# Expert layers of a diffusion trunk: row buffers handed over pair by pair from the one-hot columns, and the first eight key blocks' gates kept on the chip

## Chip, cores and metric

The kernel is one program on one core of a Trainium2 chip. The metric is the device time in microseconds (us) of one execution, as the median of several. The profile is of one execution of its own.

## What is computed

Two layers of a trunk over 640 tokens (128 context, 512 latent) of width 1024. Each layer has a mixer (not touched here) and then an expert layer with product keys:

```python
q = (xt @ w_q).reshape(n, 8, 2, 128)
s = einsum('thcd,hcnd->thcn', q, keys)            # 128 keys a side
sv, si = top_k(s, 16)                             # 16 best of each side
best, bi = top_k(sv[:, :, 0, :, None] + sv[:, :, 1, None, :], 16)   # 16 best pairs of each of 8 heads
eidx, gate = i1 * 128 + i2, softmax(best)         # 128 experts a token
act = gelu(einsum('td,ted->te', xi, u_tab[eidx])) * gate
out = einsum('te,ted->td', act, v_tab[eidx])
```

`u_tab` and `v_tab` have 16,384 rows of 1024 floats each.

## The kernel before

The five token tiles of 128 are treated in two ways. The first 320 tokens (`DENSE`) are **dense**: all 128 blocks of 128 experts pass through the chip. For each block `c`, TensorE makes the dot products (`chunk_dots`, L608), ScalarE the gelu (`gelu`, L451), VectorE multiplies by a dense table of gates (`weigh`, L899), and TensorE adds the product with the block of `v` (`chunk_sums`, L647 and L656). The last half of the third tile and two more tiles are **row tokens**: GpSimd gathers for each of their experts one row a partition (`indirect_dma_start`, L427, 512 KB for 128 partitions), 320 rows of `u` and 320 of `v` a layer. VectorE takes a dot product (`own_u`, L913) or a multiply-add (`own_v`, L938) with each. They go through a ring of ten row buffers (`RING`), tile `expert_rows`. Row `r` may be fetched once `row_used` says that row `r - 10` is used. VectorE takes 14 rows before the first `weigh`, and then some rows between the `weigh` of each two blocks, in a fixed order.

Ahead of the loop over blocks stands the **spread stage**, which makes the dense gates. For each of the 320 dense tokens, a one-hot column of the first key (by GpSimd L415, ScalarE L466 and L471, or VectorE L884, as the string `HOT_MAKERS` says) and one of the second key times the gate (VectorE L888) are multiplied on TensorE (L634). The result is [second key, first key] for one token. Columns lie in two rings of 32: the first ones in row buffers 0 to 3, the second ones in row buffers 4 to 7, so column `n` lies in buffer `(n % 32) // 8` of its four. The semaphore `spread` counts the tokens that TensorE has done. ScalarE copies eight tokens at a time out of the banks (L484). After each 16 tokens (`k` from 0 to 19) it issues a store of 1024 KB, cut into pieces of 512 bytes, to `gates_dram`, ordered by group of eight first keys (L492, called put `k` below). Its semaphores `gates_put` alternate with `k`. Before ScalarE fills a staging buffer again it waits for put `k - 2`. The tile `shared` holds both the staging buffers and, later, two read buffers for a group of eight blocks' gates.

SyncE has its queue written out in order: the blocks of `u` and `v` through six buffers (L363), and, after the first block of `v`, a wait for all puts (L372), then the reads of gate groups 0 and 1 (L374), then more blocks. While SyncE waits there, no later block is issued. `weigh(0)` waits for the read of group 0, and TensorE's `chunk_sums(0)` for `weigh(0)`. Four more blocks' dots (21 to 24) stand on TensorE between the spread and `chunk_sums(0)`. Between the spread and the 14 rows, VectorE does 40 steps of a search for the fourth tile (L721 to L796); the rest of that search is done five steps at a time after each `weigh`, and its result is what the rows of later tiles wait for (`idx_ready`).

## Time and profile before

| what | value |
|---|---|
| time, median of 3 runs | 4286.23 us (4280.3 to 4286.56) |
| profiled execution, its own time | 4284.1 us |
| its span, first to last instruction | 4282.3 us |
| TensorE busy, share of the span | 91% |
| VectorE | 71% |
| GpSimd | 45% |
| ScalarE | 16% |
| bytes moved, mean rate | 1169.31 MB, 273 GB/s |

Spread stages lie at about 895 to 1000 us (layer 0) and 2975 to 3077 us (layer 1), the block loops behind them up to about 2160 and 4240 us. An engine's busy share tells little by itself. What matters is which wait ends last at each place, and so the sections below look at single stretches.

### The profile page before, as it was taken

To read this page: it belongs to the slowest core of one execution; us is meant where nothing else is said; L and a number is where in the kernel's file an instruction comes from. 1 tells how busy PE (TensorE), PEld (TensorE's weight loads), DVE (VectorE), ACT (ScalarE), POOL (GpSimd) and SP (SyncE) were. 2 spreads that over 40 slices of the span, in tenths; PEclk is the share of its full clock that TensorE was granted. 3 is DMA by queue.
4 is the path that set the end of the run, shared out by engine and by line. 5 is a ranking of instruction groups with operands and counts; after the bars stand their busy time and mean duration, and the time that the engine had idled before them with its cause. 6 is when DMAs were issued, how large, how long until landed. Compare 5 with 4: busy or idle time off the path is not lost. (4 is left out here: it accounts for less than half of the span.)

```text
span 4282.3 us, 46161 instructions
## 1 busy us (share of the span) xinstructions
PE 3884.7 (91%) x16342; PEld 2307.9 (54%) x16342; DVE 3038.4 (71%) x6236; ACT 688.4 (16%) x1432; POOL 1910.2 (45%) x1654
## 2 busy tenths in 40 slices
PE   7986899997999899999979997999888999999897
PEld 3643656775444444444447875577744444444442
DVE  6747635888877777778763146588988777777787
ACT  4122511163000000000023122103600000000000
POOL 0002300077777677776700000003867767677673
PEclk9997899998999999999989999999999999999999
DMA  4212741269999999999922105013899999999996
GB/s 178 89 50 99 280 170 40 72 180 340 411 415 420 420 419 419 418 416 417 419 92 68 59 20 128 20 55 119 270 408 403 420 420 420 420 419 417 416 418 259
DMA packets 375715, 1169.31 MB, mean 273 GB/s; under 512 B 35833, under 2 KB 120281, under 8 KB 364042
## 3 DMA queue, kind: packets, MB, share of 16 engines
q0 software_dynamic: 184960, 679.58, 39.1%
q1 hardware_dynamic: 107856, 445.02, 27.5%
q10 hardware_dynamic: 82684, 41.95, 3.5%
q8 instruction: 122, 2.00, 0.2%
q14 instruction: 93, 0.76, 0.0%
HBM read 1116.99 MB, written 48.37 MB: 272 GB/s over the span
## 5 line engine op out<-in xcount | busy, mean ns | idle before, releaser
L608 PE MATMUL banks<-h_dense_T,blocks 128*128 128x320 f32 x4096 | 1139.1, 432 | 0.0
L656 PE MATMUL banks<-blocks,picked_T 128*128 128x512 f32 x2048 | 989.6, 627 | 0.0
L608 PEld LDWEIGHTS banks<-h_dense_T,blocks 128*128 128x128 f32 x4096 | 776.9, 190 | 387.3 <-issue 98.5
L427 POOL DMA_INDIRECT expert_rows<-in_pk_u_dram,expert x640 | 820.4, 1282 | 346.9 <-DVE own_dots L913 164.8
L938 DVE SCALAR_TENSOR_TENSOR acc<-expert_rows,expert_weight,acc 128x1024 f32<-128x1024 f32 x628 | 794.6, 1284 | 253.1 <-DMA expert_rows<-in_pk_v_dram,expert 248.0
L427 POOL DMA_INDIRECT expert_rows<-in_pk_v_dram,expert x640 | 817.3, 1277 | 327.1 <-issue 158.8
L913 DVE CUSTOM_DVE_ANT_0 expert_rows<-expert_rows,h_rows 128x1024 f32<-128x1024 f32 x640 | 773.8, 1225 | 248.3 <-DMA expert_rows<-in_pk_u_dram,expert 243.8
L656 PEld LDWEIGHTS banks<-blocks,picked_T 128*128 128x128 f32 x2048 | 384.9, 198 | 619.8 <-issue 619.8
L647 PE MATMUL banks<-blocks,picked_T 128*64 128x512 f32 x1024 | 297.1, 657 | 195.3 <-DVE picked_T L899 194.7
L451 ACT ACTIVATE dense_act<-banks 128x320 f32<-128x320 f32 x246 | 107.8, 438 | 2107.4 <-PE banks L608 2107.4
L415 POOL TENSOR_SCALAR expert_rows<-iota,picked_T 128x128 f32<-128x128 f32 x320 | 207.0, 664 | 440.0 <-ACT picked_T L457 394.4
L647 PEld LDWEIGHTS banks<-blocks,picked_T 128*64 128x64 f32 x1024 | 55.5, 139 | 327.2 <-issue 327.2
L588 PE MATMUL banks<-h_dense_T,blocks 128*128 128x384 f32 x512 | 209.7, 492 | 2.9 <-PEq L107 2.9
L899 DVE TENSOR_TENSOR picked_T<-dense_act,shared 128x320 f32<-128x320 f32 x246 | 180.7, 736 | 27.8 <-DMA shared<-gates_dram 14.6
L888 DVE TENSOR_SCALAR expert_rows<-iota,picked_T 128x128 f32<-128x128 f32 x640 | 183.7, 362 | 4.4 <-PE banks L634 4.1
L402 POOL IOTA iota<- 128x17 f32 x2 | 0.3, 157 | 404.3 <-POOLq L107 404.3
L634 PE MATMUL banks<-expert_rows 128*128 128x128 f32 x1280 | 149.9, 277 | 15.7 <-issue 9.1
L2984 POOL MEMSET VX<- 128x40 f32 x1 | 0.2, 172 | 356.9 <-POOLq L107 356.9
L634 PEld LDWEIGHTS banks<-expert_rows 128*128 128x128 f32 x1280 | 146.2, 192 | 21.1 <-issue 10.4
L2077 POOL MEMSET norm_rows<- 128x4096 f32 x1 | 3.5, 3511 | 341.1 <-POOLq L107 341.1
L590 PE MATMUL banks<-shared,blocks 128*128 128x256 f32 x512 | 153.7, 382 | 0.0
L1542 PE MATMUL banks<-HT,MIXT 128*128 128x320 f32 x512 | 142.8, 439 | 6.5 <-DMA MIXT<-in_ev_w_in_dram 6.5
(528 smaller groups left out, 3908.1 us busy)
## 6 DMA issues: line engine op xcount, KB each, us to landing
blocks<-in_pk_u_turned_dram SPq DMA_DIRECT2D x256, 512.0 KB, 6.5
blocks<-in_pk_v_dram SPq DMA_DIRECT2D x256, 512.0 KB, 6.5
ada_block<-in_ada_rest_dram SPq DMA_DIRECT2D x32, 1280.0 KB, 6.9
gates_dram<-shared ACTq DMA_DIRECT2D x40, 1024.0 KB, 5.5
shared<-gates_dram SPq DMA_DIRECT2D x32, 1280.0 KB, 10.5
blocks<-in_pk_w_q_dram SPq DMA_DIRECT2D x32, 512.0 KB, 3.5
expert_rows<-in_pk_u_dram,expert POOLq DMA_INDIRECT x640, 13.0
expert_rows<-in_pk_v_dram,expert POOLq DMA_INDIRECT x640, 13.3
```

The costliest lines, as they stand in the source:

```text
L415: pool.tensor_scalar(hot(first_hot, n), iota128[:], cols[:, z, 0, t:t + 1], None, ALU.is_equal).then_inc(hot_first, 1)
L427: pool.indirect_dma_start(out=rows[:, r % RING, :], out_offset=None, in_=table, in_offset=bass.IndirectOffsetOnAxis(ap=idx[:, at_:at_ + 1] ...
L588: pe.matmul(ps[:, at_:at_ + ND * P], lhs, HT[:, k, :], start=(k == 0), stop=(k == KD - 1))
L590: mm = pe.matmul(ps[:, at_ + HALF:at_ + HALF + NR * P], lhs, HTR[:, k, :], start=(k == 0), stop=(k == KD - 1))
L608: mm = pe.matmul(dense_dots(c), u[:, k * P:(k + 1) * P], HT[:, k, 0:DENSE], start=(k == 0), stop=(k == KD - 1))
L634: pe.matmul(ps[:, at_:at_ + P], hot(second_hot, n), hot(first_hot, n), start=True, stop=True).then_inc(spread, 1)
L647: mm = pe.matmul(ps[here:here + size, at_:at_ + width], wt[:, c % WEIGHED, token:token + size], v[:, q * width:(q + 1) * width], start=(c ...
L656: mm = pe.matmul(ps[:, at_:at_ + HALF], wt[:, c % WEIGHED, z * P:(z + 1) * P], v[:, half_ * HALF:(half_ + 1) * HALF], start=(c == 0), stop ...
L888: dve.tensor_scalar(hot(second_hot, n), iota128[:], cols[:, z, 1, t:t + 1], cols[:, z, 2, t:t + 1], ALU.is_equal, ALU.mult).then_inc(hot_s ...
L899: dve.tensor_tensor(wt[:, c % WEIGHED, :], activation_of(c), gate_of[g % 2][:, :, c % KEYS_A_GROUP], ALU.mult).then_inc(weighed, 1)
L913: dve.tensor_tensor_reduce(rows[:, r % RING, :], rows[:, r % RING, :], H[:, (u - 1) % 3, :], 1.0, 0.0, ALU.mult, ALU.add, dots[:, at_:at_ ...
L938: ins = dve.scalar_tensor_tensor(out=a, in0=rows[:, r % RING, :], scalar=by, in1=a, op0=ALU.mult, op1=ALU.add)
```

## The change

Two things are changed in both layers.

1. **Rows.** Row `r` no longer lies in buffer `r % 10` but in `SLOT_OF_ROW[r % 10]`: rows 0 and 1 in buffers 8 and 9, which never held columns, rows 2 and 3 in 0 and 4, rows 4 and 5 in 1 and 5, and so on. GpSimd's one wait for all 320 tokens of `spread` is replaced by a wait ahead of each of the pairs 2, 4, 6 and 8, for 296, 304, 312 and 320 tokens. Rows 0 and 1 have none.
2. **Gates.** Of each 16 tokens, the part for the first eight blocks (64 KB) is copied by a DMA of its own from the staging buffer into `first_gates`, on the chip; the store to `gates_dram` holds the 15 other groups. `weigh(0)` waits for all these copies (`first_put`), no longer for a read. The `weigh` of blocks 0 to 7 becomes two instructions, over 256 and 64 tokens, since the copies lie in two places. After its wait for all puts SyncE reads one group, not two.

Besides, `fold` (one small VectorE addition) is made later and lies in a tile that is free by then.

```diff
+SLOT_OF_ROW = (8, 9, 0, 4, 1, 5, 2, 6, 3, 7)
+def slot(r):
+    return SLOT_OF_ROW[r % RING]
+def hots_through(r):
+    return DENSE - HOTS + 8 * (r // 2)
...
# SyncE
                     for b in range(2):
                         sp.wait_ge(gates_put[b], 16 * batches // 2)
-                    for b in range(2):
-                        sp.dma_start(gate_in[b], gates[b].rearrange("i t j -> i (t j)")
-                                     ).then_inc(gates_got[b], 16)
+                    sp.dma_start(gate_in[0], gates[1].rearrange("i t j -> i (t j)")
+                                 ).then_inc(gates_got[0], 16)
...
# GpSimd
-            pool.wait_ge(spread, DENSE)
...
+                    if r % FREED == 0 and 0 < r < RING:
+                        pool.wait_ge(spread, hots_through(r))
                     if r % FREED == 0 and r + FREED > RING:
                         pool.wait_ge(row_used, r + FREED - RING)
                     pool.indirect_dma_start(
-                        out=rows[:, r % RING, :], out_offset=None, in_=table,
+                        out=rows[:, slot(r), :], out_offset=None, in_=table,
...
# ScalarE
                     if part == 0 and k >= 2:
                         act.wait_ge(gates_put[k % 2], 16 * (k // 2))
+                        act.wait_ge(first_put[k % 2], 16 * (k // 2))
...
                         act.wait_ge(spread_out, q + 1)
-                        act.dma_start(gates[:, :, k * BATCH:(k + 1) * BATCH, :].rearrange(
-                            "g i t j -> i g (t j)"), staged[k % 2].rearrange(
+                        held, at_ = divmod(k * BATCH, FIRST_HELD)
+                        act.dma_start(first_gates[held][:, at_ * KEYS_A_GROUP:(at_ + BATCH) * KEYS_A_GROUP],
+                                      staged[k % 2][:, 0].rearrange("p t j -> p (t j)")
+                                      ).then_inc(first_put[k % 2], 16)
+                        act.dma_start(gates[1:, :, k * BATCH:(k + 1) * BATCH, :].rearrange(
+                            "g i t j -> i g (t j)"), staged[k % 2][:, 1:].rearrange(
...
# VectorE
             def weigh(c):
                 g = c // KEYS_A_GROUP
-                if c % KEYS_A_GROUP == 0:
-                    dve.wait_ge(gates_got[g % 2], 16 * (g // 2 + 1))
+                if c == 0:
+                    for b in range(2):
+                        dve.wait_ge(first_put[b], 16 * ((batches + 1 - b) // 2))
+                elif c % KEYS_A_GROUP == 0:
+                    dve.wait_ge(gates_got[(g - 1) % 2], 16 * ((g - 1) // 2 + 1))
...
+                if g == 0:
+                    dve.tensor_tensor(wt[:, c % WEIGHED, 0:FIRST_HELD], activation_of(c)[:, 0:FIRST_HELD],
+                                      first_of[0][:, :, c], ALU.mult)
+                    dve.tensor_tensor(wt[:, c % WEIGHED, FIRST_HELD:DENSE],
+                                      activation_of(c)[:, FIRST_HELD:DENSE], first_of[1][:, :, c],
+                                      ALU.mult).then_inc(weighed, 1)
+                    return
```

How the instructions stand now, at the three places that matter. First ScalarE at the end of layer 0's spread stage, before the change (L484 copies out of the banks, L492 is a put, L451 a gelu):

```order
L484 ACTIVATE shared<-banks 128x16x64
L451 ACTIVATE acc<-banks 128x320
L492 DMA gates_dram<-shared 128x16x128
L484 ACTIVATE shared<-banks 128x16x64
L466 ACTIVATE expert_rows<-iota_0,picked_T 128x128 x4
L471 ACTIVATE expert_rows<-expert_rows,iota_0 128x512
L484 ACTIVATE shared<-banks 128x16x64
L492 DMA gates_dram<-shared 128x16x128
L484 ACTIVATE shared<-banks 128x16x64 x2
L492 DMA gates_dram<-shared 128x16x128
L451 ACTIVATE acc<-banks 128x320 x4
```

and with it:

```order
L501 ACTIVATE shared<-banks 128x16x64
L467 ACTIVATE acc<-banks 128x320
L510 DMA more_first_gates<-shared 128x128
L513 DMA gates_dram<-shared 128x15x128
L501 ACTIVATE shared<-banks 128x16x64
L482 ACTIVATE expert_rows<-iota_0,picked_T 128x128 x4
L487 ACTIVATE expert_rows<-expert_rows,iota_0 128x512
L501 ACTIVATE shared<-banks 128x16x64
L510 DMA more_first_gates<-shared 128x128
L513 DMA gates_dram<-shared 128x15x128
L501 ACTIVATE shared<-banks 128x16x64 x2
L510 DMA more_first_gates<-shared 128x128
```

Each put has a second DMA ahead of it in ScalarE's order and in its DMA queue; nothing else has moved. Next GpSimd's first row gathers behind its last column, before (semaphores bear the name of an earlier stage that used them: `ctx_out_0` and `dft_out_0` stand for `spread` and `idx_ready`, `norm_set_0` for `row_used`):

```order
L427 DMA expert_rows<-in_pk_u_dram,expert 128x1024 [waits ctx_out_0,dft_out_0]
L427 DMA expert_rows<-in_pk_u_dram,expert 128x1024 x9
L427 DMA expert_rows<-in_pk_u_dram,expert 128x1024 [waits norm_set_0]
```

and with the change (`odd_out_0` stands for `idx_ready`, `dft_out_0` for `spread`):

```order
L443 DMA expert_rows<-in_pk_u_dram,expert 128x1024 [waits odd_out_0]
L443 DMA expert_rows<-in_pk_u_dram,expert 128x1024
L443 DMA expert_rows<-in_pk_u_dram,expert 128x1024 [waits dft_out_0]
L443 DMA expert_rows<-in_pk_u_dram,expert 128x1024
L443 DMA expert_rows<-in_pk_u_dram,expert 128x1024 [waits dft_out_0]
```

The wait for `spread` stands ahead of each pair from the second, and no longer ahead of the first row. Last, VectorE behind the 14th row (L913 is a row's dot product), before:

```order
L913 ISA own_dots 128x1
L899 TENSOR_TENSOR picked_T<-dense_act,shared 128x320
L800 TENSOR_TENSOR expert_weight<-expert_weight,rest 128x128
```

and with the change:

```order
L944 ISA own_dots 128x1
L924 TENSOR_TENSOR picked_T<-dense_act,shared 128x256
L926 TENSOR_TENSOR picked_T<-dense_act,more_first_gates 128x64
L821 TENSOR_TENSOR expert_weight<-expert_weight,rest 128x128
```

`weigh(0)` keeps its place and is two instructions.

## Rows read from the trace of the kernel before

**Rows 1.** The page: the chain that ended last, by line

```profile
POOL expert_rows L427 8%; DMA expert_rows<-in_pk_v_dram,expert 7%; DMA expert_rows<-in_pk_u_dram,expert 6%; PE banks L608 2%; PE banks L588 2%; PE banks L590 1%; PE banks L634 1%; DVE expert_rows L913 1%; DMA gates_dram<-shared 1%; DVE acc L938 1%; PE banks L599 0%; PE banks L656 0%; ACT expert_rows L466 0%; DMA shared<-gates_dram 0%; DVE X L904 0%
```

**Rows 2.** The chain around layer 1's turn from spread to loop: start, us, what

```profile
3058.80 0.36 ACTq L492
...
3069.69 8.04 DMA gates_dram<-shared
...
3079.72 24.30 DMA gates_dram<-shared
3104.10 8.35 DMA shared<-gates_dram
3112.47 0.73 DVE picked_T L899
...
3177.98 11.76 DMA expert_rows<-in_pk_u_dram,expert
```

**Rows 3.** Timeline of that turn: start, us, instruction, [idle before <-releaser]

```profile
3052.08 17.66 POOL L415 TENSOR_SCALAR expert_rows<-iota,picked_T 128x128 f32<-128x128 f32 x28 [0.25 <-PE banks L634]
...
3069.49 7.31 PE L634 MATMUL banks<-expert_rows 128*128 128x128 f32 x64
...
3077.08 1.04 POOL L427 DMA_INDIRECT expert_rows<-in_pk_u_dram,expert  x1 [7.33 <-PE banks L634]
...
3083.64 1.22 DVE L913 CUSTOM_DVE_ANT_0 expert_rows<-expert_rows,h_rows 128x1024 f32<-128x1024 f32 x1 [4.23 <-DMA expert_rows<-in_pk_u_dram,expert]
...
3102.12 1.23 DVE L913 CUSTOM_DVE_ANT_0 expert_rows<-expert_rows,h_rows 128x1024 f32<-128x1024 f32 x1 [0.23 <-DMA expert_rows<-in_pk_u_dram,expert]
...
3103.43 1.22 DVE L913 CUSTOM_DVE_ANT_0 expert_rows<-expert_rows,h_rows 128x1024 f32<-128x1024 f32 x1
...
3109.49 0.94 POOL L427 DMA_INDIRECT expert_rows<-in_pk_u_dram,expert  x1 [0.31 <-issue]
3112.47 0.73 DVE L899 TENSOR_TENSOR picked_T<-dense_act,shared 128x320 f32<-128x320 f32 x1 [7.81 <-DMA shared<-gates_dram]
...
3113.35 1.98 PE L647 MATMUL banks<-blocks,picked_T 128*64 128x512 f32 x4 [19.33 <-DVE picked_T L899]
```

**Rows 4.** Windows of layer 1's loop: width, busy PE PEld DVE ACT POOL, PEclk, DMA, GB/s

```profile
3112.00:3152.00 40.00, 35.62 (x104) 17.98 (x105) 37.80 (x72) 2.60 (x4) 24.63 (x16) 0.93 0.99 389
...
3592.00:3632.00 40.00, 39.51 (x124) 20.16 (x123) 31.13 (x53) 2.19 (x5) 31.17 (x25) 1.00 1.03 420
```

**Rows 5.** The same in windows of 4 us, from 3140 on

```profile
3140.00:3144.00 4.00, 4.00 (x15) 2.48 (x14) 4.00 (x9) 0.00 (x0) 3.69 (x2) 1.00 0.94 329
3144.00:3148.00 4.00, 4.00 (x14) 1.80 (x13) 3.96 (x11) 0.44 (x1) 3.09 (x4) 1.00 0.94 352
3148.00:3152.00 4.00, 4.00 (x13) 2.25 (x13) 2.75 (x6) 0.00 (x0) 3.39 (x3) 1.00 0.91 290
```

**Rows 6.** DMA queues in the window 3079 to 3104: packets, MB, share of 16 engines

```profile
q0 software_dynamic: 2211, 8.08, 84.3%
q10 hardware_dynamic: 2732, 1.38, 18.6%
```

**Rows 7.** The put queue without rows beside it, window 3077 to 3078

```profile
q10 hardware_dynamic: 575, 0.29, 102.6%
```

**Rows 8.** Layer 0's turn, timeline

```profile
998.06 1.09 POOL L427 DMA_INDIRECT expert_rows<-in_pk_u_dram,expert  x1 [7.92 <-PE banks L634]
...
1031.98 0.74 DVE L899 TENSOR_TENSOR picked_T<-dense_act,shared 128x320 f32<-128x320 f32 x1 [6.77 <-DMA shared<-gates_dram]
```

**Rows 9.** Window of layer 1's spread stage: busy PE PEld DVE ACT POOL

```profile
2978.00:3078.00 100.00, 93.67 (x703) 85.54 (x703) 96.44 (x364) 82.59 (x159) 89.23 (x144) 1.00 0.78 221
```

**Rows 10.** Waits in that stage: engine line, releaser: us in total, times, longest

```profile
ACT shared L484 <- PE banks L634: 5.6, 8, 1.4
ACT shared L484 <- DMA gates_dram<-shared: 5.1, 4, 2.4
...
PE banks L634 <- ACT expert_rows L471: 1.7, 4, 0.8
```

More of the change, by code:

```diff
@@ L160 @@
 KEYS_A_GROUP = 8
+FIRST_HELD = 256
 GROUPS_OF_KEYS = P // KEYS_A_GROUP
 RING = 10
+SLOT_OF_ROW = (8, 9, 0, 4, 1, 5, 2, 6, 3, 7)
 FREED = 2
@@ L268, in experts @@
                "dve_line", "iota_done", "distances", "hot_by_act", "hot_by_dve", "cols_set", "cols_turned", "cols_out", "hot_first",
-               "hot_second", "spread", "spread_out", "gates_put0", "gates_put1", "gates_got0",
+               "hot_second", "spread", "spread_out", "gates_put0", "gates_put1", "first_put0", "first_put1", "gates_got0",
                "gates_got1", "dots_out", "weighed", "idx_ready", "row_used", "own_dots", "own_gelu", "own_sum", "fold_done", "fold_out",
@@ L279, in experts @@
         gates_put, gates_got = (gates_put0, gates_put1), (gates_got0, gates_got1)
+        first_put = (first_put0, first_put1)
         cand = buf(ctx, nc, "sums", [P, HEADS, 2 * P])
@@ L294, in experts @@
         own_gate = buf(ctx, nc, "own_gate", [P, OWN_STEPS])
-        fold = buf(ctx, nc, "fold", [P, OWN])
         rows = buf(ctx, nc, "expert_rows", [P, RING, D])
@@ L300, in experts @@
         root = buf(ctx, nc, "root", [P, NT])
+        more_first = buf(ctx, nc, "more_first_gates", [P, (DENSE - FIRST_HELD) * KEYS_A_GROUP])
         block = ctx.enter_context(nc.Block())
+        fold = best_of[:, 1].rearrange("p h k -> p (h k)")[:, 0:OWN]
         wt = cols[:, :, :, :].rearrange("p z a t -> p (z a t)")[:, 0:WEIGHED * DENSE].rearrange(
@@ L315, in experts @@
         gate_of = [g.rearrange("p (t j) -> p t j", j=KEYS_A_GROUP) for g in gate_in]
+        first_gates = [shared[:, 4 * D:4 * D + FIRST_HELD * KEYS_A_GROUP], more_first[:, :]]
+        first_of = [g.rearrange("p (t j) -> p t j", j=KEYS_A_GROUP) for g in first_gates]
         g_row = cand[:, :, :].rearrange("p (g h) n -> p g (h n)", g=2)
@@ L378, in _ @@
                     sp.wait_ge(weighed, KEYS_A_GROUP * (g - 1))
-                    sp.dma_start(gate_in[g % 2], gates[g].rearrange("i t j -> i (t j)")
-                                 ).then_inc(gates_got[g % 2], 16)
+                    sp.dma_start(gate_in[(g - 1) % 2], gates[g].rearrange("i t j -> i (t j)")
+                                 ).then_inc(gates_got[(g - 1) % 2], 16)
                 if c == 5 * KEYS_A_GROUP:
@@ L898, in weigh @@
                     dve.wait_ge(block_used, block_of_sums(c - WEIGHED) + 1)
-                dve.tensor_tensor(wt[:, c % WEIGHED, :], activation_of(c),
-                                  gate_of[g % 2][:, :, c % KEYS_A_GROUP], ALU.mult
+                if g == 0:
[5 more added lines that the diff above has]
+                    return
+                dve.tensor_tensor(wt[:, c % WEIGHED, 0:DENSE], activation_of(c),
+                                  gate_of[(g - 1) % 2][:, :, c % KEYS_A_GROUP], ALU.mult
                                   ).then_inc(weighed, 1)
@@ L912, in own_u @@
                     dve.wait_ge(row_in[r % RING], 16 * (r // RING + 1))
-                    dve.tensor_tensor_reduce(rows[:, r % RING, :], rows[:, r % RING, :],
+                    dve.tensor_tensor_reduce(rows[:, slot(r), :], rows[:, slot(r), :],
                                              H[:, (u - 1) % 3, :], 1.0, 0.0, ALU.mult, ALU.add,
@@ L934, in own_v @@
                     if n < 2:
-                        ins = dve.tensor_scalar(a, rows[:, r % RING, :], by, None, ALU.mult)
+                        ins = dve.tensor_scalar(a, rows[:, slot(r), :], by, None, ALU.mult)
                     else:
                         dve.wait_ge(row_used, r - 1)
-                        ins = dve.scalar_tensor_tensor(out=a, in0=rows[:, r % RING, :], scalar=by,
+                        ins = dve.scalar_tensor_tensor(out=a, in0=rows[:, slot(r), :], scalar=by,
                                                        in1=a, op0=ALU.mult, op1=ALU.add)
@@ L1004, in normalize @@
                 dve.tensor_tensor(h, h, shift[:, g, :], ALU.add).then_inc(h_ready, 1)
-            ins = dve.tensor_tensor(fold[:], ident[:, 0:OWN], ident[:, OWN:2 * OWN], ALU.add)
-            for q in range(2, WAYS):
-                line.then(ins)
-                ins = dve.tensor_tensor(fold[:], fold[:], ident[:, q * OWN:(q + 1) * OWN], ALU.add)
-            line.then(ins)
             for c in range(CODES):
@@ L1017, in _ @@
                     pass
+            ins = dve.tensor_tensor(fold[:], ident[:, 0:OWN], ident[:, OWN:2 * OWN], ALU.add)
+            for q in range(2, WAYS):
+                line.then(ins)
+                ins = dve.tensor_tensor(fold[:], fold[:], ident[:, q * OWN:(q + 1) * OWN], ALU.add)
+            line.then(ins)
             for z in range(ND):
```

2 lines of the change are left out of this document (1 added, 1 removed).

## The prediction

> **What bounds the kernel now.** I read first the page's chain of work that ended last, then its pieces at the turn from the spread stage to the loop, then the timeline, the 4 us windows and the DMA queues of that turn.
>
> The chain [rows 1] leads by shares through the row gathers (GpSimd's issues and the rows' transfers). In the middle of a loop a window shows 420 GB/s with the DMA engines at 1.03 of their time [rows 4]: there the transfers are the bound, and no engine's work counts. At the start of a loop it is otherwise. In 3112 to 3152 VectorE is busy 37.80 of 40 us [rows 4], and in 3140 to 3152 the rate falls to 329, 352 and 290 GB/s [rows 5]: the transfers have caught up with what was asked for. The chain there [rows 2] runs: the put issued at 3079.72 takes 24.30 us, the read of the gates 8.35, `weigh(0)` starts at 3112.47, then VectorE's work and GpSimd's issues follow, and only at 3177.98 the transfers. So the time of `weigh(0)` is what shifts the loop. Bytes saved before 3140 buy nothing, since the engines have idle room at 3140 anyway.
>
> At the turn [rows 3] GpSimd's last column ends at 3052.08 + 17.66 = 3069.74, and it waits 7.33 us for the spread until row 0 at 3077.08. VectorE waits 4.23 us for row 0, starts at 3083.64, and is through with the 14th row at about 3104.7. Then it waits 7.81 us for the gates. TensorE waits 19.33 us. In layer 0 the same waits are 7.92 and 6.77 us [rows 8].
>
> **The change part by part (layer 1).**
>
> *Rows earlier.* GpSimd is free at 3069.74. TensorE's last 64 products, two a token, run from 3069.49 to 3076.8, so 0.23 us a token, and row issues can come every 0.94 + 0.31 = 1.25 us [rows 3], so the pair waits hardly hold it: all of rows 0 to 9 are issued about 7.3 us earlier. Row 0 took 3083.6 - 3077.08 = 6.5 us to land. It is there at 3076.5, and VectorE, free at 3083.64 - 4.23 = 3079.41, starts without a wait. Rows in a row without a wait are 3103.43 - 3102.12 = 1.31 us apart [rows 3], so 14 take 18.3 us and VectorE reaches `weigh(0)` at 3097.8, not 3104.7. That alone is no gain: the question is whether the first gates are there.
>
> *What the rows meet.* Between 3079 and 3104 the row queue moved 2211 packets of 3.7 KB, the put queue 2732 of 0.5 KB [rows 6], some 600 of these before rows flowed and the rest, like the rows, at about 97 in a us. The queues take turns by packet, whatever its size. Alone, the put queue moves 575 packets a us [rows 7]. Before, only the last put, `k` = 19, met the rows, and it took 24.30 us. Put 17, issued at 3069.69, was through in 8.04 us [rows 2], its data moving from about 3073.5 on, since a block load stood beside it. Now rows 0 and 1, issued at 3070, have their first data at 3073. So puts 17, 18 and 19 all meet them. ScalarE can't copy out the last tokens before put 17 has landed, now at about 3090 rather than 3077.7; the copy for `k` = 19 stands in one queue behind put 18.
>
> *When the first gates land.* Rows stop when the ring is full: 14 used and 10 more, 24 in all. From 3073.3 the engines must move these, 24 x 1.27 = 30.5 us (1.46 us apart at about 0.87 of the engines' time), and puts 17, 18 and the copy of 19, 2 x 2048 + 128 = 4224 packets or 7.3 us. 37.8 us at a share of 1.04 end at 3109.7, and with about 1 us to land `weigh(0)` goes at 3110.7 rather than 3112.47: **1.8 us** gained. Taking turns by packet the copy can't be much earlier: 4224 packets at 97 a us need over 40 us, longer than the rows last. In layer 0 GpSimd is free at 998.06 - 7.92 = 990.14; the same sum gives 1031.1 against 1031.98, **0.9** gained. Bounds: 0 below, and above VectorE's own 3112.5 - 3097.8 = 14.7. I take 1.3 a layer, near the lower end, since the row that is nearest (the put of 24.30 us) is just such a transfer beside rows.
>
> The Trainium skill, page "DMA: Bandwidth & Descriptors", section "Queues, rings and completion order", says that each DMA engine goes round between the queues that have work, packet by packet. Rows 6 agree. If instead bytes were shared evenly (half of 420 GB/s for the puts), their 2.2 MB would be through in 10 us, by 3084, and `weigh(0)` would go at 3097.8. By that rule this change works against itself.
>
> *One gate read less.* Without the change of the rows this would take the 8.35 us read off the chain. With it, SyncE's wait for all puts ends about when put 19 lands, some 3.3 us after the copy, at 3114, against 3104.10. What is queued behind it (group 1's gates, `v` block 1, `u` block 26 and so on) comes 10 us later. Group 0 is no longer ahead of it. TensorE needs `v` block 1 at 3113.35 + about 11 = 3124; issued at 3114, behind 1280 KB, it lands about 3122. I cost it at nothing; the cover is 2 us, and without it TensorE, then `weigh` three blocks on, would wait.
>
> *20 more DMA issues on ScalarE.* Each put takes 0.36 and about 0.1 us in its order [rows 2], so up to 9.4 us a layer. In the stage ScalarE is busy 82.59 of 100 us [rows 9] without the puts' 7 us, and waits 10.7 us at its copies alone [rows 10], while TensorE (93.67 busy) waits for its columns only 1.7 us. One issue lies on the chain, one more ahead of the copies of `k` = 19. Bounds: 0.5 below, 9.4 above. I take **1.5 us**, near the lower end, as ScalarE's own waits are larger than what is added.
>
> *Weigh in two.* 0.73 us for 320 tokens; the second instruction adds between 0 and 0.15 us, eight times, where VectorE is busy without a gap: 0 to 1.2, I take **0.6**. The addition `fold` only moves.
>
> **Sum.** A layer: -1.3 + 1.5 + 0.6 = +0.8, both +1.6. The profiled execution's own 4284.1 us (span 4282.3 and 1.8 around it) becomes 4285.7. It lies 2.1 under the median of 4286.23, so 4288.
>
> **The rivals.**
>
> *A, faster: the first gates come in time.* If the puts get more than a packet each in turn, or puts 17 and 18 are nearly through before the rows' data flow, `weigh(0)` goes when VectorE is ready: 14.7 us earlier in layer 1. For it speaks that put 17's data began in 3073.5 too, a hair behind the rows, and that the chain ends in this very wait. Against it: rows 6. The gain isn't 14.7: then the transfers bound the loop, and they save the read (1.28 MB at 420 GB/s, 3.1 us), the idle in 3140 to 3152 (2.75 us worth) and some 0.7 us at the start, 6.5 in all; less 2.1 for ScalarE and VectorE, 4.4 a layer. About 4277, and 4271 if further dips of the loop are filled as well. It decides from `weigh(0)` at about 3106.
>
> *B, slower: ScalarE becomes the spread's bound.* If its 20 issues are paid in full, the stage is 9.4 us longer instead of 1.5; that is +7.9 a layer, 4304. From 4 us a layer on (half of the issues) the result is over the bound. For it: busy, puts and waits already fill 100 us. Against: over 10 of them are waits.
>
> *C, slower: SyncE's wait for the puts.* If put 19 lands after 3117, block 1 comes after 3125; TensorE stalls, and blocks 1 to 3 come in a burst with the rows, 3 to 5 us a layer: 4295.
>
> *D, the handover does nothing*, since GpSimd's row 2 and later wait for the spread: then only the gates part acts, `weigh(0)` at 3104.7, and the result is A's. The timeline speaks against it, GpSimd being idle 7.33 us.
>
> **How the numbers follow.** A measurement of this kernel tells about 0.2%, 8.6 us, from no change. The forecast (within 8.6 us): 0.47. A with D: 0.28, of which 0.27 over the bound. B 0.12, C 0.13, nearly all over it. So faster 0.27, same 0.48, slower 0.25. The range from 4271 (all of A but its farthest) to 4301 (C and half of B) leaves out under 2 in 10. The likeliest case's own is 4281 to 4294.
>
> **What would show it.** In the changed kernel's profile: row 0 issued within 1 us of GpSimd's last column; VectorE's first row without a wait; put 17 landing after 12 us or more rather than 8, and ScalarE waiting over 8 us for it; `weigh(0)` behind a wait of over 8 us for a DMA into the first gates, at 3108 to 3113 less shifts; SyncE's gate read about 10 us later than before. Right in mechanism and wrong in size if only the spread stage's length differs. It is wrong if `weigh(0)` follows the 14th row without a wait, or if the loop's length, from `weigh(0)` to the last row, changes by more than 3 us.

## The result, and the profile after

The changed kernel takes 4308.51 us (median of 5 runs, 4300.47 to 4315.49) against 4285.33 (5 runs, 4280.3 to 4286.56): ratio **1.0053**, 95% interval 1.0041 to 1.0064. It is slower, by more than the 0.2% that counts as a difference here, and 7.5 us above the end of the range of the prediction. Its profiled execution takes 4304.76 us, span 4303.0, against 4284.1.

The page of the changed kernel, chain by line, has the same leaders as [rows 1] and the DMA into the first gates in place of the read and the put:

```profile
DMA expert_rows<-in_pk_v_dram,expert 8%; POOL expert_rows L443 7%; DMA expert_rows<-in_pk_u_dram,expert 6%; PE banks L629 3%; PE banks L609 2%; PE banks L611 1%; PE banks L655 1%; DVE expert_rows L944 1%; DVE acc L969 1%; PE banks L677 1%; DMA more_first_gates<-shared 1%; PE banks L620 0%; ACT expert_rows L482 0%; PE banks L668 0%; ACT shared L501 0%
```

Shares don't say where 20 us went. The stages do. The column products (`spread`) begin and end the spread stage, so one line's first and last start give its length. Layer 1, before:

```profile
L634 PE MATMUL banks<-expert_rows x640: 272/275/377, 2974.2 to 3076.5; 128*128 128x128 f32 x160
```

and after:

```profile
L655 PE MATMUL banks<-expert_rows x640: 272/275/425, 2986.2 to 3100.2; 128*128 128x128 f32 x160
```

102.3 us have become 114.0; in layer 0 102.9 have become 113.6. The last start and the start of the first weighing give the turn, and that and the start of the last of VectorE's row operations the loop. From one profile each, us (before, after):

| | layer 0 | layer 1 |
|---|---|---|
| spread stage, first to last product | 102.9, 113.6 | 102.3, 114.0 |
| last product to `weigh(0)` | 34.5, 34.8 | 36.0, 34.8 |
| `weigh(0)` to the last row | 1125.0, 1124.5 | 1126.8, 1125.3 |
| first product to last row | 1262.4, 1272.9 | 1265.1, 1274.1 |

10.5 and 9.0 us, together 19.5 of the 20.7 between the two profiled executions, lie in the expert layers, and the spread stage alone has grown by more than that. The rest of a profile isn't used for such sums: the start of layer 0 lies anywhere from 894.4 to 905.7 us in the profiles, though the work ahead of it is the same, so all tables here go from a layer's first product. The profiled executions of e2 (4306.13 us) and e8 (4281.93), with the latest starts, 905.7 and 905.4, are 10 and 11 us longer than the medians of these kernels.

A window of 100 us of the spread stage after (width; busy PE, PEld, DVE, ACT, POOL; clock; DMA; GB/s), beside [rows 9]:

```profile
2989.00:3089.00 100.00, 86.31 (x627) 78.98 (x627) 87.93 (x294) 74.88 (x145) 86.35 (x140) 0.97 0.67 190
```

Every engine does less in 100 us, TensorE 86.31 instead of 93.67 and ScalarE 74.88 instead of 82.59. The waits over the whole stage, 2986.4 to 3100.5 (us in total, times, longest), beside [rows 10]:

```profile
ACT shared L501 <- PE banks L655: 12.8, 10, 1.8
ACT expert_rows L482 <- PE banks L655: 9.0, 7, 2.0
...
PE banks L655 <- issue: 7.8, 4, 2.7
PE banks L655 <- ACT expert_rows L487: 6.6, 7, 2.0
```

TensorE waits longer for ScalarE: 6.6 us, and 2.5 before over its whole stage ([rows 10] has 1.7 in its 100 us). ScalarE's rows need care. 12.8 us stand at its copies where 5.6 stood, and 9.0 at its columns where the kernel before, over its whole stage, has 2.5. But these are idle times of ScalarE, and its own DMA issues count as idle; they are put down to whatever released the next instruction. The timeline of before shows it, with an issue of 0.37 us inside an idle time of 0.50 that is put down to TensorE:

```profile
3043.68 1.00 ACT L484 ACTIVATE shared<-banks 128x1024 f32<-128x1024 f32 x1
3044.71 0.37 ACTq L492 DMA_DIRECT2D gates_dram<-shared  x1
3045.18 1.03 ACT L484 ACTIVATE shared<-banks 128x1024 f32<-128x1024 f32 x1 [0.50 <-PE banks L634]
```

and that of after, with the pair of issues:

```profile
3087.72 1.00 ACT L501 ACTIVATE shared<-banks 128x1024 f32<-128x1024 f32 x1
3088.75 0.47 ACTq L510 DMA_DIRECT2D more_first_gates<-shared  x1
3089.26 0.61 ACTq L513 DMA_DIRECT2D gates_dram<-shared  x1
3089.99 1.02 ACT L501 ACTIVATE shared<-banks 128x1024 f32<-128x1024 f32 x1 [1.27 <-PE banks L655]
```

From the end of one copy out of the banks to the start of the next it is 1.27 us where it was 0.50: 0.77 more, 20 times a layer, 15.4 us, of which 10.7 and 11.7 show in the stage. Eleven of the 16 idle times with a put in layer 1 before are 0.50 or less, and 12 of the 18 with issues after lie between 1.20 and 1.29. If the issues, and 0.13 us around one or 0.17 around a pair, are taken out of ScalarE's idle time, what is left to wait is 7.0 and 6.5 us before (layer 0, layer 1), and 3.4 and 3.5 after. So ScalarE's true waits did shrink, by some 3 us a layer; there were only 7 to begin with.

Something else comes with it. TensorE's granted clock, 1.00 through this stage before, falls to half twice a layer. Windows of the changed kernel, layer 1 (width; busy PE, PEld, DVE, ACT, POOL; clock; DMA; GB/s):

```profile
3018.00:3022.00 4.00, 1.80 (x16) 1.64 (x16) 4.00 (x15) 3.51 (x7) 4.00 (x8) 1.00 0.90 246
3022.00:3026.00 4.00, 4.00 (x23) 4.00 (x23) 4.00 (x14) 3.15 (x7) 4.00 (x7) 0.57 0.75 211
...
3042.00:3046.00 4.00, 1.27 (x12) 1.11 (x11) 4.00 (x15) 3.81 (x7) 4.00 (x8) 0.99 0.87 244
3046.00:3050.00 4.00, 4.00 (x16) 3.40 (x16) 3.27 (x11) 2.71 (x6) 3.10 (x5) 0.58 0.65 183
```

The full level is 2.4 GHz and the lower one 1.2 GHz. Just ahead of these two falls TensorE stood idle for 2.20 and 2.73 us; before, none of its waits in the stage was over 1.5. For the same products TensorE is then busy 99.9 and 99.6 us a stage, not 95.5 and 95.2. Its busy time has grown by 4.3 us in each layer, and the rest of the stage's growth, 6.4 and 7.4 us, is idle time of TensorE.

At the turn (timeline of the changed kernel):

```profile
3092.55 1.04 POOL L443 DMA_INDIRECT expert_rows<-in_pk_u_dram,expert  x1 [0.17 <-issue]
...
3094.37 0.61 ACTq L513 DMA_DIRECT2D gates_dram<-shared  x1
...
3099.11 7.29 ACTq L510 DMA_DIRECT2D more_first_gates<-shared  x1
...
3099.83 1.22 DVE L944 CUSTOM_DVE_ANT_0 expert_rows<-expert_rows,h_rows 128x1024 f32<-128x1024 f32 x1
...
3120.00 1.94 ACT L501 ACTIVATE shared<-banks 128x1024 f32<-128x1024 f32 x2 [20.91 <-DMA gates_dram<-shared]
...
3121.97 5.20 ACTq L510 DMA_DIRECT2D more_first_gates<-shared  x1
3127.20 1.24 ACTq L513 DMA_DIRECT2D gates_dram<-shared  x1
...
3135.01 0.63 DVE L924 TENSOR_TENSOR picked_T<-dense_act,shared 128x256 f32<-128x256 f32 x1 [14.62 <-issue]
...
3137.86 0.33 SPq L389 DMA_DIRECT2D shared<-gates_dram  x1
```

Row 0 leaves 0.17 us behind GpSimd's last column and VectorE takes it without a wait. But put 17, issued at 3094.37, 1.8 us behind row 0, lands 25.6 us later. ScalarE's last two copies wait 20.91 us for it, the copy of the gates for `k` = 19 goes at 3121.97, and VectorE, ready at 3120.4, waits 14.62 us (the profile names no releaser there; `weigh(0)` stands behind the waits for `first_put`). The two copies on the chip also show 7.29 and 5.20 us in their issue instead of 0.47. The queues of the changed kernel from 3100 to 3110 (packets, MB, share):

```profile
q0 software_dynamic: 914, 3.35, 82.3%
q10 hardware_dynamic: 1297, 0.66, 22.0%
```

The puts get some 130 packets a us beside the rows, as against 575 alone [rows 7]. From 3110 to 3120 the two queues move 992 packets each, so 99 a us for the puts.

### The profile page after: what moved, and what is told of

Its sections match the earlier page's. It is cut to its first block and busy times, and to the rows that moved or that the text cites. A ratio compares the mean times of both kernels' runs of the same rounds, so it can differ in the third digit from the quotient of the medians.

```text
span 4303.0 us, 46215 instructions
## 1 busy us (share of the span) xinstructions
PE 3892.3 (90%) x16342; PEld 2315.8 (54%) x16342; DVE 3039.1 (71%) x6252; ACT 686.3 (16%) x1432; POOL 1911.0 (44%) x1654
## 5 line engine op out<-in xcount | busy, mean ns | idle before, releaser
L909 DVE TENSOR_SCALAR expert_rows<-iota,picked_T 128x128 f32<-128x128 f32 x640 | 183.7, 362 | 17.6 <-PE banks L655 17.5
L930 DVE TENSOR_TENSOR picked_T<-dense_act,shared 128x320 f32<-128x320 f32 x230 | 168.6, 735 | 12.7 <-PE banks L677 12.3
## 6 DMA issues: line engine op xcount, KB each, us to landing
shared<-gates_dram SPq DMA_DIRECT2D x30, 1280.0 KB, 10.5
expert_rows<-in_pk_u_dram,expert POOLq DMA_INDIRECT x640, 12.8
```

Of the source, the lines that this page charges most:

```text
L909: dve.tensor_scalar(hot(second_hot, n), iota128[:], cols[:, z, 1, t:t + 1], cols[:, z, 2, t:t + 1], ALU.is_equal, ALU.mult).then_inc(hot_s ...
L930: dve.tensor_tensor(wt[:, c % WEIGHED, 0:DENSE], activation_of(c), gate_of[(g - 1) % 2][:, :, c % KEYS_A_GROUP], ALU.mult).then_inc(weighe ...
```

## The experiments

Theory T at the outset: the time went to ScalarE's issues; the early rows only give back what the held gates gain. Rivals: the cost is in the rows, or in the transfers.

Each ratio is to the kernel before timed beside that run (its medians lie between 4284.12 and 4286.26 us). "Stage", "turn" and "loop" are the three stretches of the table above, layer 0 / layer 1.

| kernel | stage | turn | loop | median us (runs) | ratio, 95% |
|---|---|---|---|---|---|
| before | 102.9 / 102.3 | 34.5 / 36.0 | 1125.0 / 1126.8 | 4285.33 | 1 |
| after | 113.6 / 114.0 | 34.8 / 34.8 | 1124.5 / 1125.3 | 4308.51 (5) | 1.0053, 1.0041 to 1.0064 |
| e1 put in two, ScalarE | 108.1 / 106.6 | 36.7 / 36.7 | 1127.8 / 1125.2 | 4304.38 (6) | 1.0041, 1.0027 to 1.0054 |
| e2 gates alone | 113.7 / 112.8 | 28.3 / 28.3 | 1129.5 / 1127.0 | 4296.08 (12) | 1.0026, 1.0015 to 1.0037 |
| e3 rows alone | 102.8 / 102.6 | 43.4 / 43.4 | 1125.7 / 1124.9 | 4302.75 (6) | 1.0038, 1.0025 to 1.0051 |
| e4 gates alone, issued by SyncE | 100.5 / 100.2 | 28.0 / 28.0 | 1127.8 / 1127.1 | 4275.54 (7) | 0.9969, 0.9954 to 0.9984 |
| e5 both, issued by SyncE | 103.2 / 100.8 | 28.4 / 26.7 | 1128.2 / 1129.3 | 4274.96 (9) | 0.9976, 0.9966 to 0.9986 |
| e6 before, puts by SyncE | 99.0 / 98.7 | 34.1 / 31.1 | 1128.5 / 1128.7 | 4277.78 (11) | 0.9984, 0.9975 to 0.9993 |
| e7 gates alone, copies by SyncE | 103.1 / 102.3 | 28.6 / 27.4 | 1126.4 / 1126.8 | 4274.24 (11) | 0.9975, 0.9966 to 0.9984 |
| e8 e5, two rows early | 100.8 / 100.1 | 25.0 / 25.5 | 1131.0 / 1131.0 | 4270.96 (7) | 0.9967, 0.9956 to 0.9978 |
| e9 e5, block ahead of put 17 | 100.9 / 100.6 | 28.6 / 27.4 | 1128.7 / 1126.7 | 4276.01 (11) | 0.9981, 0.9971 to 0.9990 |
| e10 both, copies by SyncE | 103.0 / 102.4 | 23.9 / 23.4 | 1132.6 / 1130.9 | 4279.05 (11) | 0.9980, 0.9971 to 0.9989 |
| e11 after, rows 0 and 1 later | 113.1 / 112.8 | 28.0 / 27.7 | 1129.5 / 1131.0 | 4297.72 (9) | 1.0033, 1.0021 to 1.0045 |

### e1: the put of the kernel before in two DMAs

```diff
-act.dma_start(gates[:, ...], staged[k % 2])         .then_inc(gates_put[k % 2], 16)
+act.dma_start(gates[0, ...], staged[k % 2][:, 0])   .then_inc(first_put[k % 2], 16)
+act.dma_start(gates[1:, ...], staged[k % 2][:, 1:]) .then_inc(gates_put[k % 2], 16)
```

> The kernel before, with each of ScalarE's 20 puts a layer cut into two DMAs, both to the gates in memory: the first group's 64 KB, then the other 15 groups. Same bytes, same read of group 0, rows as before. Theory T (ScalarE's longer issue time stretches the spread stage): each put now holds ScalarE about 0.75 us longer, the stage from the first column product to the last grows from 100.8 to about 112 us in layer 1 and likewise in layer 0, and the time is 4305 to 4309 us. Rival R (the rows' early start and its contention cost the time; the issues are hidden behind ScalarE's waits): stage within 2 us of before, time within 4 us of before, 4282 to 4289.

The issues on ScalarE, layer 0 (shortest/median/longest ns, first and last start):

```profile
L495 ACTq DMA_DIRECT2D gates_dram<-shared x20: 325/326/363, 907.7 to 1010.9; - x20
L498 ACTq DMA_DIRECT2D gates_dram<-shared x20: 443/453/1669, 908.1 to 1011.3; - x20
```

Layer 1 has the same medians, 326 and 454. 0.33 and 0.45 us stand where 0.37 stood, 0.41 more, 8.3 us in twenty, and with what lies between and around them ScalarE's idle time at a put goes from 0.50 to 0.96, 9.2 us in twenty. The stage is 5.2 and 4.3 us longer, 106.6 us in layer 1 where I had expected 112, and the kernel 18 us slower, though bytes, targets, rows and weighing are those of before. Of ScalarE's waits beyond issues 3.4 and 1.2 us are left. The clock falls once in layer 0's stage (0.76 and 0.81 from 954 to 962) and not in layer 1's, though TensorE's longest wait is 1.9 us in both. One more issue for each put, and nothing else, is enough to make it slower. It costs less than in the changed kernel because the pair there is longer (0.47 and 0.61). The three stretches hold 13.6 of the 18 us; the profiled layer 0 starts 5.6 us later than before's, which no edit of e1 touches.

### e2 and e3: each part alone

e2 is the changed kernel with the old wait ahead of row 0:

```diff
+pool.wait_ge(spread, DENSE)
 for phase in PHASES:
...
-if r % FREED == 0 and 0 < r < RING:
-    pool.wait_ge(spread, hots_through(r))
```

> The changed kernel with GpSimd's one wait for all 320 tokens put back ahead of row 0: the gates part alone. Theory T: the stage is 11 to 12 us longer as in the changed kernel, but the first gates' last copy is not behind rows, so weigh(0) follows the 14th row at once, 7 to 8 us earlier against the end of the stage than before; per layer about +11.5 - 7.3 + 0.6, so +8 to +10 us in all, 4293 to 4296. Rival R (early rows are the loss): faster than before by the two waits of 7.8 and 6.8 us, 4271 to 4275.

e3 is the kernel before with the new slots and the pair waits, its puts untouched:

```diff
-pool.wait_ge(spread, DENSE)
...
+if r % FREED == 0 and 0 < r < RING:
+    pool.wait_ge(spread, hots_through(r))
...
-out=rows[:, r % RING, :], ...
+out=rows[:, slot(r), :], ...
```

> The kernel before with the new slots and the pair waits alone: gates written and read as before. Theory T: the stage keeps its 100.8 us; puts 17 to 19 meet the rows, ScalarE waits over 15 us for put 17, all puts land about 10 us later against the end of the stage (as in the changed kernel), and the read of group 0 follows behind that, so weigh(0) is 7 to 10 us later; 4299 to 4305. Rival R2 (starting rows early costs nothing, the engines only move the same bytes in another order): 4280 to 4288.

The stage is long in e2 (113.7 and 112.8) and unchanged in e3 (102.8 and 102.6): it belongs to the gates part. The turn shortens by 6.2 and 7.7 us in e2, where VectorE goes from its 14th row to `weigh(0)` with no wait at all, and lengthens by 8.9 and 7.4 us in e3. There the read still stands on the path, behind the last put. ScalarE waits 13.3 and 8.0 us for put 17, not the 15 and more expected. Timeline of e3:

```profile
3100.49 4.85 ACTq L504 DMA_DIRECT2D gates_dram<-shared  x1
```

```profile
3135.05 0.73 DVE L911 TENSOR_TENSOR picked_T<-dense_act,shared 128x320 f32<-128x320 f32 x1 [20.99 <-DMA shared<-gates_dram]
```

Rows that leave earlier delay the puts, and what waits for the puts pays. Both parts alone are slower than before, for different reasons, and in the changed kernel the turn (34.8) lies between the two.

### e4, e6, e7: the issues taken off ScalarE

e6 is the kernel before with its puts on SyncE, whose own loads are put between them in the order in which they stood; e4 is e2 with both DMAs of a put on SyncE; in e7 SyncE issues only the copy, and the store stays on ScalarE.

```diff
 # e4; e6 has the one whole put here, e7 only the first of the two
+def put(k):
+    sp.wait_ge(spread_out, 2 * k + 2)
+    sp.dma_start(first_gates[held][...], staged[k % 2][:, 0]).then_inc(first_put[k % 2], 16)
+    sp.dma_start(gates[1:, ...], staged[k % 2][:, 1:]).then_inc(gates_put[k % 2], 16)
+for k in range(batches):
+    put(k)
+    for q, what in zip(GAPS, later):
+        if (q - 1) // 2 == k:
+            load(*what)
```

> The gates part alone, with both DMAs of each 16 tokens issued by SyncE instead of ScalarE (between its block loads, in an order that keeps each load where its buffer comes free); ScalarE issues nothing in the stage. Theory T: the issue time leaves ScalarE, 0.5 us a put less than even before, so the stage is 0 to 5 us shorter than the 100.8 us of before, and weigh(0) follows the 14th row at once: 10 us a layer gained less the 0.6 of the cut weigh, 4264 to 4274. Rival R3 (the stage is longer because of the copy itself or the cut store of 15 groups, whoever issues them): stage near 112 us and 4290 to 4297.

> The kernel before with its one put of 16 groups for each 16 tokens issued by SyncE instead of ScalarE; nothing held on the chip, rows as before. Theory T: ScalarE is relieved of about 0.5 us a put, the stage is some 2 us shorter as in e4, weigh(0) still waits for all puts and the read, 36.0 us (layer 1) and 34.5 us (layer 0) after the last column product: 2 to 3 us a layer, 4279 to 4284. Rival (the whole gain of e4 is ScalarE's relief): 4271 to 4277.

> The gates part alone, with only the 64 KB copies issued by SyncE; ScalarE keeps the store of 15 groups. It separates the issue on ScalarE from the copy. Theory T: a store without a DMA just ahead of it holds ScalarE 0.37 to 0.45 us, the stage is 102 to 104.5 us (102.3 before, 112.8 with both on ScalarE), weigh(0) 28.3 us after it: 4272 to 4280. Rival (the copies' traffic or the second wait ahead of the staging buffer stretch the stage): stage over 108 us, 4288 or more.

The product rows of layer 1, of e4:

```profile
L664 PE MATMUL banks<-expert_rows x640: 273/276/378, 2979.5 to 3079.7; 128*128 128x128 f32 x160
```

of e6:

```profile
L644 PE MATMUL banks<-expert_rows x640: 273/275/377, 2976.5 to 3075.2; 128*128 128x128 f32 x160
```

and of e7, with its store on ScalarE:

```profile
L666 PE MATMUL banks<-expert_rows x640: 273/275/377, 2971.7 to 3074.0; 128*128 128x128 f32 x160
...
L524 ACTq DMA_DIRECT2D gates_dram<-shared x20: 371/381/426, 2979.2 to 3076.5; - x20
```

The stage follows what ScalarE issues. Per put on ScalarE, beside before: nothing (e4, e6), stage 2.1 to 3.9 us shorter; 0.38 us (e7), within 0.2; 0.33 and 0.45 (e1), 4.3 to 5.2 longer; 0.47 and 0.61 (after, e2), 10.5 to 11.7 longer. The bytes and the number of DMAs are the same in e2, e4 and e7, and e7 keeps the second wait ahead of the staging buffer, so that neither the copies' traffic nor that wait is the cause. In e4 and e6, with no issue on it, ScalarE waits 12 to 14 us: there its work is no longer what sets the stage. All three, e4, e6 and e7, are faster than before, e6 by 0.16% only, under the 0.2% taken above; at 4277.78 us it is just outside both ranges written down for it, and e4's 4275.54 is 1.5 us above its own. e4 against e2, the same work on another queue, is 20.5 us.

### e5 and e10: the whole change without its price on ScalarE

e5 is the changed kernel with both DMAs of a put on SyncE, as e4; e10 with only the copies there, as e7.

> The changed kernel in full, but both DMAs of each 16 tokens are issued by SyncE as in e4: so e4 plus the rows' early start. Theory T (the row part costs because rows and puts take turns by packet): the stage is as short as in e4 (100.2 us in layer 1), but puts 17 and 18 meet the rows again, and weigh(0) comes about 34.8 us after the last column product as in the changed kernel, not 28.0 as in e4; so 6 to 7 us a layer slower than e4, 4284 to 4291. Rival (the row part only hurts together with ScalarE's longer issues, since its issues block behind a full queue): weigh(0) within 2 us of e4's and the time 4268 to 4276, VectorE starting its rows 4 us earlier.

> The changed kernel in full, with only the 64 KB copies issued by SyncE and the 15-group puts left on ScalarE (e7 plus the rows' early start). Theory T2: the stage is 102 to 104 us as in e7; put 17 stands beside the block load and is caught by the rows, 13 to 20 us to land, and ScalarE waits for it; but the last copy is not in the queue behind put 18 any more, so it lands some 3 us after ScalarE's last copy out of the banks, and weigh(0) comes 24 to 27 us after the last product, when VectorE is through with 14 rows: 4269 to 4277. Rival (the copy must wait its turn among the rows for as long as in the changed kernel): weigh(0) 33 us or more after the last product, 4286 to 4292.

Stage as in e4 and e7 but for layer 0 of e5, turn 26.7 to 28.4 us in e5 and 23.9 and 23.4 in e10, 4275 and 4279 us (e10 2 us above its range): the full change is faster than before as soon as ScalarE is rid of the extra issues. But I had expected e5 to beat e4, and it doesn't; the early rows bring nothing measurable (0.9976 against 0.9969, and 0.9980 against 0.9975 for e10 against e7). For e5 the three stretches give 5.0 us against e4, and 3.3 of them lie in the stage: the clock falls once in its layer 0 (0.86 and 0.71 from 918 to 926), and that stage takes 103.2 us against 100.8 in layer 1. The rest, and all of it for e10, is in the loop. e10 starts weighing 11 to 13 us earlier than before and needs 7.6 and 4.1 us more from there to the last row. The waits of e10 in the first 200 us of layer 1's loop:

```profile
PE banks L680 <- DMA blocks<-in_pk_v_dram: 14.6, 1, 14.6
```

SyncE's wait for the puts stands ahead of `v` block 1. The gate read goes at 3123.1 in e10 and 3120.0 in e5 (e4 3107.8), the block behind it, and TensorE stands still for 14.6 and 8.6 us. This is rival C's mechanism, which I had costed at nothing; in the changed kernel itself no such wait shows, since there `weigh(0)` is late too.

e10 has the earliest `weigh(0)` of all although its put 17 is caught by the rows: it is issued 0.42 and 0.09 us behind row 0, takes 17.5 and 12.4 us, and ScalarE waits 11.8 and 6.7 us for it. But the last copy goes on SyncE's queue, not behind put 18, and VectorE comes to `weigh(0)` without a wait. In e5, where both are in one queue, VectorE waits 4.3 and 3.2 us.

### e8: only rows 0 and 1 early

```diff
 def hots_through(r):
-    return DENSE - HOTS + 8 * (r // 2)
+    return DENSE
```

(on e5, so that rows 2 and later wait for all products)

> e4 plus only rows 0 and 1 (buffers 8 and 9, which held no columns) fetched before the spread is through; row 2 waits for all 320 tokens. Theory T: two rows are 2.6 us of transfers beside put 17, which lands 2 to 3 us later, without the crawl of a full ring; VectorE starts row 0 about 4 us earlier, waits for row 2 until it lands as in e4, and is through with row 13 about 3 us earlier, so 2 to 3 us a layer faster than e4: 4268 to 4272. Rival (any row beside the puts starves them for as long as the ring is fed): weigh(0) 30 us or more after the last column product and no faster than e4, 4275 to 4282.

Turn 25.0 and 25.5, 4270.96 us, **0.9967** (0.9956 to 0.9978): the lowest median of all. Its loop too gives back 4 to 6 us, with TensorE's wait for `v` block 1 at 11.2 and 12.6 us. By their intervals e8, e4, e7 and e5 can't be told from each other; each beats both kernels.

### e9 and e11: why put 17 is so slow in the changed kernel

In e5 put 17 lands in 6.7 and 5.9 us, in the changed kernel in 26.4 and 25.6. Two candidates: the block load of SyncE that stands beside it, or that it is issued behind row 0. e9 moves the load ahead of the put (on e5):

```diff
 for k in range(batches):
+    if k == 17:
+        load(*later[-1])
     put(k)
```

> e5 with one swap in SyncE's order: the load of a block of u that stood behind put 17 stands ahead of it. In e5 put 17 was through in 6 us, before the rows' data flowed, and weigh(0) came 26.7 us (layer 1) and 28.4 us (layer 0) after the last column product; in the changed kernel put 17 went 6 us before the last product, beside that block, was caught by the rows and took 26 us, and ScalarE waited 21 us for it. Theory T2 (what costs is put 17 being caught by the rows, which its place against the block decides): put 17 now takes 14 us or more, ScalarE waits 8 us or more for it, the copy of the last tokens goes later and weigh(0) comes 31 to 35 us after the last product; 4280 to 4288. Rival (the order doesn't matter; the rows only hurt together with ScalarE's longer pair of issues): within 2 us of e5 at weigh(0), 4271 to 4279.

Put 17 takes 9.8 and 8.6 us, not 14 or more, the turn is 28.6 and 27.4: as in e5. The order of the load is not what makes put 17 late, and that idea of mine fell.

e11 is the changed kernel with its first two rows held to the wait of row 2, by the profiles 4.1 and 3.3 us later beside the last product. ScalarE's issues stay.

```diff
-if r % FREED == 0 and 0 < r < RING:
-    pool.wait_ge(spread, hots_through(r))
+if r % FREED == 0 and r < RING:
+    pool.wait_ge(spread, max(hots_through(r), hots_through(2)))
```

> The changed kernel, but rows 0 and 1 wait for the same column product as row 2 (the eighth after the first slots come free), so that row 0 is issued about 2.8 us later, behind put 17's store and no longer 1.8 to 2.5 us ahead of it. Everything on ScalarE stays as in the changed kernel, so the stage from the first to the last column product should again last 113 to 115 us. Theory T3 (the early rows take the end of the puts only because ScalarE's longer issues set put 17 behind row 0; in the runs with SyncE's issues it was ahead and landed in 6 to 17 us): put 17 lands in under 12 us instead of 25.6, the first weighing starts 27 to 31 us after the last product instead of 34.8, the time is 4296 to 4303 us. Rival R3 (the late first weighing comes of the puts and rows sharing the queues as such, whichever is first): the first weighing stays at 33 to 36 us, the time at 4305 to 4312 us.

In layer 1 row 0 now leaves 1.5 us behind put 17 instead of 1.8 ahead. Queues of e11 from 3099 to 3100, before the rows' data, and from 3101 to 3102, with them:

```profile
q10 hardware_dynamic: 660, 0.34, 113.3%
```

```profile
q0 software_dynamic: 48, 0.20, 83.2%
q10 hardware_dynamic: 117, 0.06, 22.9%
```

Put 17's data are nearly through when the rows' begin, and it lands in 6.8 and 6.5 us; the last two copies follow at 3102.41 instead of 3120.00:

```profile
3102.41 1.94 ACT L501 ACTIVATE shared<-banks 128x1024 f32<-128x1024 f32 x2 [1.84 <-DMA gates_dram<-shared]
```

The stage stays at 113.1 and 112.8, the turn falls from 34.8 to 28.0 and 27.7, the time to 4297.72. All numbers of the theory hold: 3 to 4 us in the order of two issues are 7 us of turn in each layer. TensorE then waits 8.5 and 10.6 us for `v` block 1, so 5.0 and 5.7 of the 7 go back in the loop by the profiles, which leaves 4.9 us for both layers. The medians are 10.8 apart, but the two were not timed together, and the intervals of their ratios just touch (1.0041 to 1.0064, 1.0021 to 1.0045): of the time itself only the direction is likely, and what lies outside the stretches stays open.

The other runs fit in between. Put 17's time to landing, by how long after row 0 it is issued (us; negative is ahead of it):

| run, layer | issued after row 0 | lands in |
|---|---|---|
| after, 0 / 1 | 2.46 / 1.82 | 26.4 / 25.6 |
| e10, 0 / 1 | 0.42 / 0.09 | 17.5 / 12.4 |
| e3, 0 / 1 | 0.36 / -0.25 | 19.0 / 13.6 |
| e9, 0 / 1 | 0.37 / -0.13 | 9.8 / 8.6 |
| e5, 0 / 1 | -0.99 / -1.08 | 6.7 / 5.9 |
| e8, 0 / 1 | -1.45 / -1.88 | 5.9 / 6.4 |
| e11, 0 / 1 | -1.62 / -1.53 | 6.8 / 6.5 |

e9, whose block load is ahead of the put, is quicker than e3 and e10 at the same distance; no run separates why.

## Why the prediction was wrong

**The step that failed: "20 more DMA issues on ScalarE", taken at 1.5 us a layer.** It measured 10.7 and 11.7, above even its upper bound of 9.4. Rival B, ScalarE as the spread's bound (4304, chance 0.12), is what happened. Three errors:

- *The size of one.* I priced the added copy like a put of before, 0.36 and 0.1. The rows show 0.47 for the copy and 0.61 instead of 0.37 for the store once it follows a copy (0.38 in e7, where it stands alone): with the time around them 0.77 in all, 15.4 us a layer. The bound should have covered that adding an issue also changes the price of its neighbour.
- *The cover.* "ScalarE's own waits are larger than what is added." The 10.7 us read from [rows 10] as waits at the copies had the puts' own 7 us of issues in them, and these were then counted a second time, beside "busy 82.59 of 100 us without the puts' 7 us". Beyond its issues ScalarE had 7.0 and 6.5 us to wait, and 15.4 were added. The changed kernel used up 3.6 and 3.0 of these 7, e1 3.6 and 5.3. That TensorE waits for ScalarE only 1.7 us told little, since both engines were nearly full: TensorE 93.67 of 100 us [rows 9], and ScalarE 82.59 with another 10 for 20 puts at 0.50.
- *The clock.* It was in no term. With long waits of TensorE its clock falls to half, twice a layer in the changed kernel, in e2 and in e11, once in layer 0 of e1 and of e5, and never in this stage in the others or before. A price comes from the two single falls: the stages of e1 take 108.1 us with it and 106.6 without, those of e5 103.2 and 100.8. At e1's 1.5 us, where ScalarE is as full as in the changed kernel, two falls are an estimated 3 of the 10.7 and 11.7 us, and the 3.4 and 3.5 us that ScalarE still waits there are the most that they can be. No run holds the clock and changes the issues alone; this share is read from the profiles, not shown by an experiment.

That the issues on ScalarE are the cause is shown by e1, e2, e4 and e7. With ScalarE's 7.3 us of puts gone the stage gave only 2.1 to 3.9 back (e4, e6), as TensorE, busy for 94 to 95 us, was close behind.

The other terms, a layer:

- *Rows earlier and first gates, -1.3 (0.9 and 1.8).* Measured beside the last product: +0.3 and -1.2. The size was near, and every sign named for it was there: row 0 within 1 us of the last column (0.17), VectorE's first row without a wait, ScalarE's wait for put 17 over 8 us (20.9), VectorE's for the first gates over 8 (14.6). But the working named the wrong cause in part. It held that the rows must meet puts 17 to 19 in any case, and that the copy in one queue behind put 18 can't be much earlier. e5 and e11 show that the first is a matter of 3 to 4 us in the order of put 17 and row 0: put 17 took 26.4 and 25.6 us, rather than the 20 worked out, when it was behind row 0, and 5.9 to 6.8 ahead of it. e10 shows that the second hangs on the queue: with the last copy on SyncE's, `weigh(0)` came 11 us earlier although the rows caught put 17. The gates alone give 6.2 and 7.7 (e2). So that the turn stayed near its old length was a matter of order and queue, not a limit of the transfers; that it came out within 2 us of the forecast is in part luck.
- *The turns between the queues.* The Trainium skill, page "DMA: Bandwidth & Descriptors", section "Queues, rings and completion order", has the DMA engines go round between queues by packet. The trace agrees: 992 packets of each queue from 3110 to 3120, and some 130 and 117 packets of the puts a us beside the rows' first data, 575 to 660 without. By that rule it pays to have a queue of small packets empty before the rows start, as e11 shows.
- *SyncE's wait, costed at nothing.* Nothing it was in the changed kernel (gate read at 3137.86, 37.7 us after the last product where it was 27.6, 10 later as predicted, and no wait of TensorE behind it). With the early turns of e5, e8, e9, e10 and e11 it costs TensorE 8.5 to 14.6 us once a layer: the cover was the late `weigh(0)` itself.
- *Weigh in two, +0.6.* 0.62 and 0.27 us for 0.73: +0.15 eight times, the upper bound. The loop is 0.5 and 1.5 us shorter all the same; nothing of it shows.
- *Rival A's size.* It had 6.5 us a layer as all that an early `weigh(0)` can give, since the transfers bind later. e10 gives 3.0 and 8.5: 10.6 and 12.6 us earlier, 7.6 and 4.1 given back in the loop. The order is right; part of what is given back is the wait for `v` block 1, which the 6.5 did not have.

The three stretches' differences, layer by layer: (10.7 + 0.3 - 0.5) + (11.7 - 1.2 - 1.5) = 19.5 of the 20.7 us.

## What to carry to other kernels

Before you call an engine's idle time in a stage cover for added work, take its own DMA issues out of it: the profile counts them as idle and puts them down to another engine. Here 14 us of idle time were 7 us of cover. Price an added issue by the idle time around it, not by its duration alone, and include what it does to the issue next to it. Where TensorE then waits longer, look at its granted clock in short windows. Put additional DMA issues on a queue whose engine does nothing else in that stage: the same change went from 1.0053 (1.0041 to 1.0064) to 0.9976 (0.9966 to 0.9986) by that, with SyncE's own loads put between. When a transfer is let start earlier, look at which small-packet transfer is issued within a few us of it, and let that one go first.

## What was not expected of the hardware

- The time that a DMA's issue takes on ScalarE's queue depends on its neighbour: the same 15-group store 0.38 us alone and 0.61 behind a copy within the chip; two stores to DRAM 0.33 and 0.45. On SyncE the pair takes 0.47 and 0.60 as well (e5), there at no cost.
- An issue lasted long when transfers were behind. In e5, layer 1, timeline of SyncE's queue:

```profile
3080.77 0.47 SPq L386 DMA_DIRECT2D more_first_gates<-shared  x1
3081.28 0.60 SPq L389 DMA_DIRECT2D gates_dram<-shared  x1
...
3083.25 9.50 SPq L386 DMA_DIRECT2D more_first_gates<-shared  x1
```

  The first pair while the queue moves, the next copy 2 us behind the store of put 18. In the changed kernel 7.29 and 5.20 us of this kind stood on ScalarE. What limits the queue there no run separates.
